# Moving layer 1's two gate groups of modulation tiles out of layer 0's output stage

## The chip, the cores and the metric

One core of one Trainium2 chip runs one launch of the kernel. The time is device microseconds of that core. TensorE (PE) multiplies, ScalarE (ACT) and VectorE (DVE) read PSUM and prepare operands, GpSimd (POOL) adds a few sums, and SyncE (SP) issues the weight transfers.

## What is computed

The reference has two blocks. The first has two layers with this skeleton, of which the change touches the modulation:

```
for l in range(2):
    m = silu(c) @ ada_w[l] + ada_b[l]          # 1024 -> 3072: shift, scale, gate
    sh, sc, gt = split(m, 3)
    h = rms_norm(x, norm_pre[l]) * (1 + sc) + sh
    z = h @ w_in[l]                            # q, k, v, hyena, gmlp, gates
    y_a = differential attention(q, k, v) with axial rope
    y_b, y_c = hyena long convolution, gmlp
    out = (sum of sel_i * (gated_i @ w_branch[i])) @ w_out[l]
    x = x + gt * rms_norm(out, norm_post[l])
```

x has 256 tokens of 1024 features; a context of 256 tokens is carried through layer 0 as well, and layer 1 still makes keys and values from it. The modulation is a product of two vectors (c and c_ctx) with a 1024 x 3072 matrix. The second block (sparse attentions, a feed-forward part, a last gated projection) comes after both layers.

## The kernel before

**The stream of tiles.** All weights lie in one array of tiles of 128 x 1024 fp32 (512 KB) in the order in which they are used. `plan()` names each tile (kind, layer, index, PSUM banks), and each engine's program walks the same list. SP loads tile t into one of four slots (`raw`, slot t mod 4). A tile of ordinary weights is split: ACT copies it to `whi` (L1194), DVE makes `wlo = raw - whi` (L1711), and PE does three matmuls for each product (L417 to L419). ACT runs three tiles ahead of its own reading of results, DVE two. A slot is free for tile t when tile t-4 has its `wlo`:

```
elif t >= second:
    sp.wait_ge(*self.at("used" if self.tiles[t - RAW].kind == "ada" else "tile_lo", t - RAW))
sp.dma_start(self.raw_tile(t), self.ins["stream"][t])
```

SP works in the order of the stream, so that a tile that waits holds back all behind it.

**Modulation tiles** (kind "ada") are used raw by PE, without a split (L506: the two vectors are the weights, the tile is the moving operand). Four tiles make one group g of 512 of the 3072 columns; groups 0 and 1 are the shift, 2 and 3 the scale, 4 and 5 the gate. When the fourth is done, ACT copies the bank to `rows` (L1217), PE transposes it (`pe_turn`, L598), and DVE adds the strips into `mod` (`dve_turned`, L1837). When groups 4 and 5 are there, `dve_mod_gate` (L2159, L2160) finishes the gate, which layer 1 needs only in its own output stage.

**Layer 0's output stage** walks eight "wout" tiles, each of 24 matmuls of 512 columns. Behind tiles 0 and 1 come two tiles each of layer 1's group 4, behind tiles 3 and 4 two each of group 5 (`WOUT_ADA`), and `pe_turn` follows at tiles 2 and 5. The same stage holds the filter of layer 1: two hidden products (L656), the taps (L666), and DVE's and ACT's part of it.

**Between the layers** (`pe_cross`, `act_cross`, `dve_cross`): PE sums the squares of the new x (L748), ACT takes the root, DVE the reciprocal (L2223), and then h comes k by k (eight k) over three steps: DVE L2238, ACT L1505 (`h_hi`), DVE L2244 (`h`). PE multiplies four query tiles by it (`pe_cross_queries`) as the k arrive, and then four key tiles over both halves. DVE does the `wlo` of the third query tile at the head of this stage and that of the fourth in `dve_cross_h(0)`, after its fourth h sum (`if s == 0 and k == 3: self.dve_lo()`); those of the four key tiles come after it.

**Layer 1's attention**: DVE turns keys and queries (`dve_rope`, L1976 to L1979) in three parts, with one `dve_tiles(1)` after each, PE does scores of unit 0 (L816), DVE the maxima (L1984 to L1986), ACT the exponentials (`act_exps`, L1387), and then eight units go on, each with two "hy" tiles of 24 matmuls of 256 columns in between. ACT takes each such result out at L1244, DVE finishes it at L1729 and L1730, and only then does the weights of the unit (L1997 to L2002), which PE transposes (L842).

Of the kernel before, what the change touches and what calls it, by code (L numbers as in the profile page):

```python
# [41 lines left out]
WOUT_ADA = {0: (4, (0, 1)), 1: (4, (2, 3)), 3: (5, (0, 1)), 4: (5, (2, 3))}  # L42
# [52 lines left out]
def plan():  # L95
# [33 lines left out]
    for l in range(DEPTH):  # L129
        n = ALL if l == 0 else TOK  # L130
        if l == 0:
            for g in FRONT_ADA:
                ada(0, g)
        for kind in ("q", "k") if l else ("k", "q"):
# [86 lines left out]
class Kernel:  # L221
    SLOTS = [0, 1, 2, 3, 6, 7] + list(range(8, 16))
    SPREAD = (4, 5, 10, 11, 12, 13)
    FRONT_GROUPS = tuple((0, g) for g in FRONT_ADA)
    LATE_ADA = ((0, 4), (0, 5), (1, 0), (1, 1))
# [259 lines left out]
    def pe_tile(self, T):  # L485
# [8 lines left out]
        if kind == "ada":  # L494
# [4 lines left out]
            if q == 0 and (T.l, g) in ASIDE:  # L499
# [87 lines left out]
    def pe_turn(self, l, g):  # L587

        pe, rows = self.pe, self.rows(l, g)
        if (l, g) in ASIDE:  # L590
            b = self.M[3]
            if (l, g) == ASIDE[1]:
                pe.wait_ge(*self.at("turned", *ASIDE[0]))
        else:
# [5 lines left out]

    def ada_bank(self, T):
        return self.M[2] if (T.l, T.j[0]) in ASIDE else self.G[T.use % 4]
# [181 lines left out]
    def pe_cross(self):  # L784

        queries, keys = self.tiles[self.pe_next:self.pe_next + 4], self.tiles[self.pe_next + 4:self.pe_next + 8]
# [32 lines left out]
    def pe_attention(self, l):  # L819
        pe, units = self.pe, self.units(l)  # L820
        n = len(units)
        pe.wait_ge(*self.at("roped", l, 7))
        self.pe_scores(l, 0)
        self.pe_tiles(1)
        for u in range(n):
# [24 lines left out]
            if i == 1:  # L850
                pe.wait_ge(*self.at("wt", l, u))
                if u == 1:
                    pe.wait_ge(*self.at("evac", self.tiles[self.first["v", l]].use + 3))
                if u > 1:
# [79 lines left out]
    def pe_block1(self, l):  # L934
# [15 lines left out]
        for o in range(KT):  # L950
            self.pe_tiles(1)
            if l == 0 and o in (2, 5):
                self.pe_turn(1, 4 + o // 3)
            if l == 0 and o in WOUT_ADA:
                self.pe_tiles(2)
# [231 lines left out]
    def act_hi(self):  # L1187

        t, act = self.act_next, self.act
        if t < len(self.tiles) and self.tiles[t].kind != "ada":  # L1190
            act.wait_ge(*self.raw_landed(t))
            if t >= FRONT + SPLIT:
                act.wait_ge(*self.at("used", t - SPLIT))
# [10 lines left out]
    def act_tile(self, T):  # L1204
        act, kind, l, j, n = self.act, T.kind, T.l, T.j, T.n
        b = self.G[T.use % 4]
        if kind == "ada":
            g, q = j
            if q == 3:
# [109 lines left out]

    def act_down_low(self, i):  # L1320
# [181 lines left out]
    def act_cross_h(self, s):  # L1502
        for k in range(KT):
            self.act.wait_ge(*self.at("h_sum", 1, s, k))
            self.act.activation(self.hi(k, s), self.tmp[:, (0, 1, 3, 4)[k % 4], self.half(s)], ACT.Identity, bias=self.mods[1][:, k, s:s + 1]).then_inc(*self.mark("act_half", "h_hi", 1, s, k))  # L1505

    def act_cross(self):
# [6 lines left out]
        self.act_hi()  # L1514
# [8 lines left out]
        for i in range(4):  # L1523
            for k in CROSS_SQ[i]:
                self.act_cross_sq(1, k)
            self.act_tiles(1)
        act.wait_ge(*self.at("summed", ("res", 0, 1), KT - 1))
# [3 lines left out]
    def act_block1(self, l):  # L1531
# [23 lines left out]
        for o in range(KT):  # L1555
            if o == 5 - 4 * l:
                act.activation(self.stat[:, 38:39], self.c["eps"], ACT.Sqrt, bias=self.c["zero"])
            self.act_tiles(3 if l == 0 and o in WOUT_ADA else 1)
# [273 lines left out]
    def dve_turned(self, l, g):  # L1832
        aside = (l, g) in ASIDE
        bank = self.M[3] if aside else self.G[self.extra["ada", l, g] % 4]
# [153 lines left out]
    def dve_attention(self, l):  # L1988
# [4 lines left out]
        self.dve_tiles(1)  # L1993
        for u in range(n):
# [12 lines left out]
            if l:  # L2007
                self.dve_tiles(FILL[1][u])
            elif u % 2:
# [145 lines left out]
    def dve_mod_gate(self, l):  # L2155

        v, mod, b = self.dve, self.mods[l], self.both(f"ada_b{l}", 24)
        v.wait_ge(*self.at("evac", self.extra["ada", l, 5]))
# [87 lines left out]
    def dve_cross(self):  # L2246
# [12 lines left out]
        for _ in range(4):  # L2259
# [5 lines left out]
    def dve_block1(self, l):  # L2265
        v, n = self.dve, TOK if l else ALL
        if l:
            self.dve_tiles(6, split=False)
# [26 lines left out]
        for o in range(KT):  # L2295
            self.dve_tiles(3 if l == 0 and o in WOUT_ADA else 1)
            if l == 0 and o in (0, 2):
                self.dve_hidden(1, o // 2)
            if l == 0 and o in (2, 5):
                self.dve_turned(1, 4 + o // 3)  # L2300
            if l == 0 and o == 5:
# [3 lines left out]
                self.dve_mod_gate(1)  # L2305
# [496 lines left out]
```

## Time and profile before

| | us |
|---|---|
| median of 3 runs (1432.98 to 1436.71) | 1434.15 |
| profiled execution, its own time | 1432.28 |
| its span, first to last instruction | 1431.0 |
| PE busy | 1374.4 (96%) |
| DVE busy | 936.4 (65%) |
| ACT busy | 686.8 (48%) |
| mean granted TensorE clock | 0.987 |

The profiled execution took 1.3 us more than its span, and the median of the runs is 1.9 us above it. In a row of the timeline stand start, duration, engine, line and operation, what it writes and reads, how many in a row, and in brackets the idle time before it and what ended that. PE's matmuls overlap, so that the distance from start to start tells what one costs, and not its duration.

### The profile page before, as it was taken

Reading aid. Unit: us, or ns where it says so; the run is one execution under the profiler, and the core shown is the slowest. Engines: PE = TensorE matmul, PEld = TensorE weight load, DVE = VectorE, ACT = ScalarE, POOL = GpSimd, SP = SyncE. Lnnn points to the kernel's source line nnn. Section 1 sums busy time; section 2 is a strip of 40 time slices with the busy share of each in tenths; the row PEclk is TensorE's granted clock in tenths of the full one; section 3 lists DMA queues with packets and bytes.
Section 4 is the critical chain, followed back from the end, with each engine's and each line's share of the span. In section 5 each row is a group of like instructions: output and inputs, shape, how many; then the busy total and the mean of one; then the engine's idle time right before and its main releaser. Section 6 shows DMA issues by size and latency. Waiting matters only on the chain.

```text
span 1431.0 us, 20879 instructions
## 1 busy us (share of the span) xinstructions
PE 1374.4 (96%) x8316; PEld 1162.7 (81%) x8316; DVE 936.4 (65%) x1688; ACT 686.8 (48%) x1190; POOL 41.6 (3%) x50
## 2 busy tenths in 40 slices
PE   6999999999999999989999999988999999999998
PEld 3676677778888887669789899987889989888878
DVE  6564664876333434398876787657877777888556
ACT  5434554134322232545455454455556746666445
POOL 0000000000000000200000000010000002000001
PEclk9999999999999999999999999998999999999999
DMA  9431351254322233513234455544543345555552
GB/s 366 169 103 59 139 197 48 71 176 144 103 90 101 91 106 104 193 59 104 88 119 133 155 174 191 180 163 137 191 133 119 104 149 175 192 191 192 198 170 74
DMA packets 57937, 202.21 MB, mean 141 GB/s; under 512 B 6288, under 2 KB 9680, under 8 KB 57840
## 3 DMA queue, kind: packets, MB, share of 16 engines
q1 hardware_dynamic: 55712, 194.27, 40.1%
q0 software_dynamic: 1760, 6.12, 1.3%
q8 instruction: 66, 1.08, 0.3%
q10 hardware_dynamic: 368, 0.48, 0.1%
q14 instruction: 31, 0.25, 0.1%
HBM read 199.80 MB, written 1.05 MB: 140 GB/s over the span
## 4 chain that ended last, share of the span: by engine, by line
PE 83%; DVE 10%; ACT 3%; DMA 2%; issue 1%; SPq 0%; DVEq 0%; ACTq 0%
PE gemm_bank L417 16%; PE gemm_bank L418 15%; PE gemm_bank L419 15%; PE misc_bank L417 4%; PE misc_bank L418 4%; PE misc_bank L419 4%; PE misc_bank L428 3%; PE gemm_bank L428 3%; DVE wlo L1711 2%; PE gemm_bank L573 1%; PE misc_bank L429 1%; PE gemm_bank L429 1%; PE misc_bank L573 1%; PE misc_bank L857 1%; PE gemm_bank L506 1%; PE misc_bank L816 1%
## 5 line engine op out<-in xcount | busy, mean ns | idle before, releaser
L1711 DVE TENSOR_TENSOR wlo<-raw,whi 128x1024 fp32r<-128x1024 f32 x316 | 383.1, 1223 | 74.6 <-ACT whi L1194 71.2
L1194 ACT ACTIVATE whi<-raw 128x1024 fp32r<-128x1024 f32 x316 | 332.6, 1055 | 163.3 <-PE gemm_bank L419 95.9
L417 PE MATMUL gemm_bank<-halves,wlo 128*128 128x256 f32 (+1 forms) x1152 | 376.4, 327 | 16.9 <-DVE halves L2244 4.2
L418 PE MATMUL gemm_bank<-halves,whi 128*128 128x256 f32 (+1 forms) x1152 | 361.4, 314 | 0.0
L419 PE MATMUL gemm_bank<-halves,whi 128*128 128x256 f32 (+1 forms) x1152 | 361.1, 313 | 0.0
L417 PEld LDWEIGHTS gemm_bank<-halves,wlo 128*128 128x128 f32 x1152 | 223.5, 194 | 40.6 <-issue 17.3
L419 PEld LDWEIGHTS gemm_bank<-halves,whi 128*128 128x128 f32 x1152 | 223.9, 194 | 12.0
L418 PEld LDWEIGHTS gemm_bank<-halves,whi 128*128 128x128 f32 x1152 | 224.2, 195 | 11.1 <-issue 0.7
L417 PE MATMUL gemm_bank<-arena_r,wlo 128*128 128x512 f32 (+1 forms) x320 | 108.4, 339 | 0.9 <-DVE wlo L1711 0.9
L419 PE MATMUL gemm_bank<-arena_r,whi 128*128 128x512 f32 (+1 forms) x320 | 107.8, 337 | 0.0
L418 PE MATMUL gemm_bank<-arena_r,whi 128*128 128x512 f32 (+1 forms) x320 | 107.8, 337 | 0.0
L417 PE MATMUL misc_bank<-halves,wlo 128*128 128x512 f32 (+1 forms) x288 | 102.0, 354 | 0.0
L418 PE MATMUL misc_bank<-halves,whi 128*128 128x512 f32 (+1 forms) x288 | 102.0, 354 | 0.0
L419 PE MATMUL misc_bank<-halves,whi 128*128 128x512 f32 (+1 forms) x288 | 102.0, 354 | 0.0
L1746 DVE SCALAR_TENSOR_TENSOR tmp<-tmp,gemm_bank 128x512 f32<-128x512 f32 (+1 forms) x28 | 16.1, 574 | 97.3 <-ACT tmp L1263 97.3
L1263 ACT ACTIVATE tmp<-misc_bank 128x512 f32<-128x512 f32 (+1 forms) x36 | 19.0, 527 | 121.4 <-PE misc_bank L419 121.4
L417 PEld LDWEIGHTS gemm_bank<-arena_r,wlo 128*128 128x128 f32 x320 | 60.8, 190 | 10.2 <-DVE wlo L1711 2.6
L419 PEld LDWEIGHTS gemm_bank<-arena_r,whi 128*128 128x128 f32 x320 | 60.8, 190 | 6.3
L418 PEld LDWEIGHTS gemm_bank<-arena_r,whi 128*128 128x128 f32 x320 | 60.8, 190 | 6.1
L428 PE MATMUL gemm_bank<-halves,whi 128*128 128x512 f32 x176 | 62.2, 395 | 0.0
L428 PE MATMUL misc_bank<-halves,whi 128*128 128x512 f32 x176 | 62.1, 394 | 0.0
L418 PEld LDWEIGHTS misc_bank<-halves,whi 128*128 128x128 f32 x288 | 54.6, 189 | 7.5
(417 smaller groups left out, 2261.5 us busy)
## 6 DMA issues: line engine op xcount, KB each, us to landing
raw<-in_stream SPq DMA_DIRECT2D x348, 512.0 KB, 3.3
arena<-in_stream SPq DMA_DIRECT2D x16, 512.0 KB, 12.6
x<-in_x SPq DMA_DIRECT2D x1, 1024.0 KB, 6.5
x<-in_ctx SPq DMA_DIRECT2D x1, 1024.0 KB, 9.4
y<-in_hy_decay POOLq DMA_DIRECT2D x2, 512.0 KB, 4.2
arena<-in_gm_ws POOLq DMA_DIRECT2D x2, 512.0 KB, 6.5
const_b<-in_const_b POOLq DMA_DIRECT2D x1, 635.0 KB, 6.3
y<-in_hy_w POOLq DMA_DIRECT2D x2, 256.0 KB, 3.7
```

Source lines behind the costliest of these rows:

```text
L417: mm(out, w_lo, r_hi, start=first, stop=False)
L418: mm(out, w_hi, r_lo, start=False, stop=False)
L419: return mm(out, w_hi, r_hi, start=False, stop=last)
L428: self.pe.matmul(bank[:, :], hi[:, c], self.hi_lo(k, s), start=(k == 0), stop=False)
L429: m = self.pe.matmul(bank[:, 0:TOK], lo[:, c], self.hi(k, s), start=False, stop=(k == KT - 1))
L506: m = pe.matmul(bank[c:c + 32, :], self.cond_w[:, 2 * q + kk, :], raw[:, kk * BR:(kk + 1) * BR], start=(q < 2), stop=(q >= 2), tile_positi ...
L573: pe.matmul(self.out_banks[o][:, :], hi[:, c], self.ah_al[:, j, :], start=(j == 0), stop=False)
L816: mm = pe.matmul(self.M[m][:, 0:nkeys], self.Q[r, h, q], self.K[r, h, k_off:k_off + nkeys], start=True, stop=True)
L1194: act.activation(self.whi[:, t % SPLIT, :], self.raw_tile(t), ACT.Copy).then_inc(*self.mark("tile_hi", "tile_hi", t))
L1263: act.activation(self.tmp[:, e % 2, 0:n], self.M[e][:, 0:n], ACT.Tanh, scale=0.5).then_inc(*self.mark("act_sel", "sel_tanh", T.use))
L1711: dve.tensor_tensor(self.wlo[:, t % SPLIT, :], self.raw_tile(t), self.whi[:, t % SPLIT, :].bitcast(F32), ALU.subtract).then_inc(*self.mark ...
L1746: self.own(dve.scalar_tensor_tensor(th, th, 1.0, b[:, 0:n], ALU.add, ALU.mult))
```

## The change

The pattern of `WOUT_ADA` (eight modulation tiles) goes. Group (1, 4), now `CROSS_ADA`, stands in the stream behind the four query tiles of layer 1 and before its keys. PE does its four tiles between the first sums and the queries, ACT copies the bank in `act_cross_h(0)` after the fourth `h_hi`, PE turns it after the keys, DVE reduces it after the second part of the rope. Group (1, 5), now `SCORE_ADA`, stands behind the value tiles: three tiles before the first hy tile, the fourth behind it. PE does three before it waits for the rope, and the fourth between the scores of unit 0 and the first hy tile; then it turns the group. ACT copies that bank after the exponentials of unit 0. DVE reduces it in unit 0 and then does the gate. Both groups are turned through misc banks. ACT's and DVE's look-ahead steps count the new places.

```
-WOUT_ADA = {0: (4, (0, 1)), 1: (4, (2, 3)), 3: (5, (0, 1)), 4: (5, (2, 3))}
+CROSS_ADA, SCORE_ADA, SCORE_ADA_LEAD = (1, 4), (1, 5), 3
...
+            if l and kind == "q":
+                for q in range(4):
+                    add("ada", 1, (CROSS_ADA[1], q), 0, 0)
+                    tiles[-1].use = cross_use
         rows("v", l, 4, ALL)
+        if l:
+            for q in range(SCORE_ADA_LEAD):
+                add("ada", 1, (SCORE_ADA[1], q), 0, 0)
         for m in range(12):
             add("hy", l, m, n, 1)
+            if l and m == 0:
+                for q in range(SCORE_ADA_LEAD, 4):
+                    add("ada", 1, (SCORE_ADA[1], q), 0, 0)
...
             add("wout", l, o, n, 1)
-            if l == 0 and o in WOUT_ADA:
-                ada_part(1, *WOUT_ADA[o])
...
     def pe_cross(self):
...
         for k in range(KT):
             self.pe_cross_sum(0, k)
+        for T in moving:
+            self.pe_tile(T)
         self.pe_cross_queries(queries)
         for i, side in CROSS_KEYS:
             self.pe_cross_keys(keys[i], side, (i, side) == (0, 1))
-        self.pe_next += 8
+        self.pe_turn(*CROSS_ADA)
+        self.pe_next += 12
...
     def pe_attention(self, l):
+        if l:
+            self.pe_tiles(SCORE_ADA_LEAD)
+        if l:
+            pe.wait_ge(*self.at("turned", *CROSS_ADA))
         pe.wait_ge(*self.at("roped", l, 7))
         self.pe_scores(l, 0)
-        self.pe_tiles(1)
+        if l:
+            lead = self.tiles[self.pe_next]
+            for T in self.tiles[self.pe_next + 1:self.pe_next + 5 - SCORE_ADA_LEAD]:
+                self.pe_tile(T)
+            self.pe_tile(lead)
+            self.pe_next += 5 - SCORE_ADA_LEAD
+            self.pe_turn(*SCORE_ADA)
+        else:
+            self.pe_tiles(1)
...
+    def act_beside(self, l, g):
+
+        T = next(T for T in self.tiles if T.kind == "ada" and T.l == l and T.j == (g, 3))
+        self.act.wait_ge(*self.at("used", T.t))
+        self.act.wait_ge(*self.at("ada_turn", l, g - 1))
+        m = self.act.activation(self.rows(l, g), self.ada_bank(T)[:, :], ACT.Copy)
...
     def act_attention(self, l):
+        if l:
+            for _ in range(3):
+                self.act_hi()
+            self.act_tiles(SCORE_ADA_LEAD, split=False)
         self.act_exps(l, 0)
-        self.act_tiles(1)
+        if l:
+            self.act_beside(*SCORE_ADA)
+            self.act_tiles(2)
+        else:
+            self.act_tiles(1)
...
             self.act.activation(self.hi(k, s), self.tmp[:, (0, 1, 3, 4)[k % 4], self.half(s)], ACT.Identity, bias=self.mods[1][:, k, s:s + 1]).then_inc(*self.mark("act_half", "h_hi", 1, s, k))
+            if s == 0 and k == 3:
+                self.act_beside(*CROSS_ADA)
...
     def dve_attention(self, l):
         self.dve_maxima(l, 0)
         self.dve_tiles(1)
+        if l:
+            self.dve_tiles(4 - SCORE_ADA_LEAD, split=False)
...
             if l:
                 self.dve_tiles(FILL[1][u])
+                if u == 0:
+                    for _ in range(4 - SCORE_ADA_LEAD):
+                        self.dve_lo()
+                    self.dve_turned(*SCORE_ADA)
+                    self.dve_mod_gate(1)
...
     def dve_block1(self, l):
             self.dve_rope(l, a, b)
+            if l and a == 3:
+                self.dve_turned(*CROSS_ADA)
             self.dve_tiles(1)
...
-        if l == 0:
-            self.dve_tiles(1)
+        self.dve_tiles(SCORE_ADA_LEAD if l else 1)
```

## Rows read from the trace of the kernel before

**Rows 1.** The page: span, and the chain that ended last by engine

```profile
span 1431.0 us, 20879 instructions
...
PE 83%; DVE 10%; ACT 3%; DMA 2%; issue 1%; SPq 0%; DVEq 0%; ACTq 0%
```

**Rows 2.** Timeline of PE in layer 0's output stage

```profile
566.97 1.06 PE L506 MATMUL gemm_bank<-raw,cond_w 128*32 128x512 f32 x8
567.96 0.64 PE L656 MATMUL misc_bank<-const_b 33*64 33x256 f32 x2
...
574.20 1.07 PE L506 MATMUL gemm_bank<-raw,cond_w 128*32 128x512 f32 x8
576.17 0.50 PE L417 MATMUL gemm_bank<-arena_r,wlo 128*128 128x512 f32 x1 [0.91 <-DVE wlo L1711]
...
581.75 0.60 PE L598 MATMUL gemm_bank<-const_a 128*128 128x128 f32 x4
```

**Rows 3.** Timeline of PE between the layers

```profile
623.41 5.37 PE L748 MATMUL misc_bank<-tmp,const_a 128*128 128x256 f32 x16
632.93 0.55 PE L417 MATMUL gemm_bank<-halves,wlo 128*128 128x256 f32 x1 [4.15 <-DVE halves L2244]
...
637.87 0.42 PE L418 MATMUL gemm_bank<-halves,whi 128*128 128x256 f32 x1
...
638.24 0.28 PE L417 MATMUL gemm_bank<-halves,wlo 128*128 128x256 f32 x1
```

**Rows 4.** Timeline of DVE between the layers

```profile
617.35 1.22 DVE L1711 TENSOR_TENSOR wlo<-raw,whi 128x1024 fp32r<-128x1024 f32 x1
...
633.89 1.22 DVE L1711 TENSOR_TENSOR wlo<-raw,whi 128x1024 fp32r<-128x1024 f32 x1
```

**Rows 5.** Windows: PE busy, its granted clock, DMA share, GB/s

```profile
622.00:624.00 2.00, 2.00 (x7) 1.00 0.00 0
...
634.00:636.00 2.00, 2.00 (x11) 0.50 0.00 0
636.00:638.00 2.00, 2.00 (x11) 0.50 0.82 268
```

**Rows 6.** All transfers into the raw slots, 560 to 740 us

```profile
DMA to landing us min/median/max: 3.1/3.7/7.3
```

**Rows 7.** The chain that ended last, near 568 us

```profile
568.43 5.35 DMA raw<-in_stream
```

**Rows 8.** Timeline of ACT between the layers

```profile
635.94 0.51 ACT L1505 ACTIVATE halves<-tmp,mod 128x256 fp32r<-128x256 f32 x1 [1.42 <-DVE tmp L2238]
```

**Rows 9.** Timeline of PE at layer 1's first scores

```profile
698.79 1.32 PE L816 MATMUL misc_bank<-arena 64*128 64x512 f32 x4 [3.44 <-DVE arena L1979]
```

**Rows 10.** Timeline of DVE: a strip sum, then around layer 1's first units

```profile
586.75 0.17 DVE L1837 TENSOR_REDUCE mod<-gemm_bank 128x8 f32<-128x32 f32 x1
...
691.26 1.22 DVE L1711 TENSOR_TENSOR wlo<-raw,whi 128x1024 fp32r<-128x1024 f32 x1
...
713.93 0.48 DVE L1729 SCALAR_TENSOR_TENSOR arena<-gemm_bank,const_b,arena 128x255 f32<-128x255 f32 x1 [1.79 <-ACT arena L1244]
```

**Rows 11.** Timeline of ACT: output stage, then layer 1's first units

```profile
577.09 0.60 ACT L1217 ACTIVATE const_a<-gemm_bank 128x512 f32<-128x512 f32 x1
577.71 1.28 ACT L1335 ACT_TABLE_LOAD   x1
579.00 0.42 ACT L1335 ACTIVATE tmp<-tmp 64x256 f32<-64x256 f32 x1
...
698.86 1.28 ACT L1387 ACT_TABLE_LOAD   x1
701.75 0.69 ACT L1387 ACTIVATE tmp<-misc_bank,stat 128x512 f32<-128x512 f32 x1 [1.60 <-DVE stat L1986]
...
703.09 1.05 ACT L1194 ACTIVATE whi<-raw 128x1024 fp32r<-128x1024 f32 x1
...
711.05 0.69 ACT L1387 ACTIVATE tmp<-misc_bank,stat 128x512 f32<-128x512 f32 x1 [1.41 <-DVE stat L1986]
```

More of the change, by code:

```diff
@@ L133, in plan @@
                 ada(0, g)
+        if l:
+            cross_use, uses = uses, uses + 1
         for kind in ("q", "k") if l else ("k", "q"):
@@ L498, in pe_tile @@
             raw, bank = self.raw_tile(T.t), self.ada_bank(T)
-            if q == 0 and (T.l, g) in ASIDE:
+            if q == 0 and (T.l, g) == SCORE_ADA:
+                pe.wait_ge(*self.at("kern", 1, 1))
+            elif q == 0 and (T.l, g) in ASIDE:
                 if (T.l, g) == ASIDE[1]:
@@ L784, in pe_cross @@
     def pe_cross(self):
-        queries, keys = self.tiles[self.pe_next:self.pe_next + 4], self.tiles[self.pe_next + 4:self.pe_next + 8]
+        queries, moving, keys = (self.tiles[self.pe_next + 4 * i:self.pe_next + 4 * i + 4] for i in range(3))
         for k in range(KT):
             self.pe_cross_sum(0, k)
+        for T in moving:
+            self.pe_tile(T)
         self.pe_cross_queries(queries)
@@ L1192, in act_hi @@
             if t >= FRONT + SPLIT:
-                act.wait_ge(*self.at("used", t - SPLIT))
+                held = t - SPLIT
+                while held > FRONT + SPLIT and self.tiles[held].kind == "ada":
+                    held -= SPLIT
+                act.wait_ge(*self.at("used", held))
             act.activation(self.whi[:, t % SPLIT, :], self.raw_tile(t), ACT.Copy).then_inc(*self.mark("tile_hi", "tile_hi", t))
@@ L1208, in act_tile @@
             g, q = j
-            if q == 3:
+            if q == 3 and (l, g) not in self.BESIDE:
                 act.wait_ge(*self.at("used", T.t))
@@ L1318, in act_tile @@
             act.activation(self.y[:, j, 0:TOK], self.y[:, j, 0:TOK], ACT.Tanh, scale=0.5).then_inc(*self.mark("act_ple", "ple_tanh", j))
+    def act_beside(self, l, g):
[3 more added lines that the diff above has]
+        m = self.act.activation(self.rows(l, g), self.ada_bank(T)[:, :], ACT.Copy)
+        if (l, g) == SCORE_ADA:
+            m.then_inc(*self.mark("act_rows", "rows", l, g))
+            return
+        m.then_inc(*self.mark("act_evac", "evac", T.use))
+        self.also("rows", l, g)
     def act_down_low(self, i):
@@ L1513, in act_cross @@
         self.act_tap_root(1)
-        self.act_hi()
+        for _ in range(5):
+            self.act_hi()
         for k in range(KT):
@@ L1557, in act_block1 @@
                 act.activation(self.stat[:, 38:39], self.c["eps"], ACT.Sqrt, bias=self.c["zero"])
-            self.act_tiles(3 if l == 0 and o in WOUT_ADA else 1)
+            self.act_tiles(1)
             if l == 0 and o in (1, 3):
@@ L1833, in dve_turned @@
         aside = (l, g) in ASIDE
-        bank = self.M[3] if aside else self.G[self.extra["ada", l, g] % 4]
+        aside = aside or (l, g) in self.BESIDE
+        bank = self.turn_bank(l, g) if aside else self.G[self.extra["ada", l, g] % 4]
         self.dve.wait_ge(*self.at("ada_turn", l, g))
@@ L2258, in dve_cross @@
             self.dve_cross_new(1, k)
-        for _ in range(4):
+        for _ in range(8):
             self.dve_lo()
@@ L2650, in _layout @@
             tiles.append(_columns(w[:, c:c + 512]))
+            if l and c:
+                ada(1, CROSS_ADA[1], CROSS_ADA[1] + 1)
         tiles.append(_rows(w[:, 512:1024]))
@@ L2661, in _layout @@
         else:
-            tiles.append(hy)
+            at = len(tiles)
+            ada(1, SCORE_ADA[1], SCORE_ADA[1] + 1)
+            moving = tiles.pop(at)
+            tiles += [moving[:SCORE_ADA_LEAD], hy[0:1], moving[SCORE_ADA_LEAD:], hy[1:]]
             early = _columns(w[:, 5632:5632 + 2 * KEPT_SEL * P])
@@ L2679, in _layout @@
         wout = _columns(i["w_out"][l])
-        if l == 0:
-            at = len(tiles)
-            ada(1, 4, 6)
-            both, done = tiles.pop(at), 0
-            for o in range(KT):
-                tiles.append(wout[o:o + 1])
-                if o in WOUT_ADA:
-                    tiles.append(both[done:done + 2])
-                    done += 2
-        else:
-            tiles.append(wout)
+        tiles.append(wout)
     w = i["w_in_2"][0]
```

30 lines of the change are left out of this document (20 added, 10 removed).

## The prediction

> **What bounds the kernel now.** I read the page first. PE has 83% of the chain that ended last [rows 1] and 96% of the span: what PE need not do, or need not wait for, is what counts. The eight moved tiles are PE work, and they still have to be done. So the change can only gain by putting them where PE stands idle, and the next views are timelines of PE at the place they leave and at the two places they go to. They leave layer 0's output stage, where PE runs without a gap but for one of 0.91 us [rows 2]. Between the layers PE stands for 4.15 us from 628.78 us on, until DVE has the first h [rows 3], and then runs at half its clock up to about 638.1 us: the granted clock is 0.50 of 2.4 GHz, that is the 1.2 GHz level [rows 5], and matmuls come every 0.21 us instead of every 0.12. At layer 1's first scores PE stands for 3.44 us, until the rope is done [rows 9]. Last I looked at what the moved steps wait for at the new places: DVE's order between the layers [rows 4], the transfers [rows 5 to 7], and ACT and DVE around the first units of the attention [rows 10, 11]. The reader is to see that both gaps are large enough for the work, and that the transfers are not ready for them.
>
> **What the output stage gives back.** One pair of tiles takes 0.99 us from its start to the start of what follows, another 1.06 us and then 0.91 us of waiting for a `wlo`, which is late because transfers of three tiles come in a bunch behind the pair (5.35 us for the last of them) [rows 2, 7]. Four pairs are 4.2 us, the wait 0.9, the two turns 0.45 each (0.60 us long, of which the last part lies under the next matmul), and each return to the weight tiles about 0.1 (the first matmul of one takes 0.50 us), five times. Sum 6.5 us; bounds 5.6 (the wait comes back in another form) and 6.8 (turns at their full length). DVE's and ACT's filter work of this stage only becomes less crowded. I take 6.5 off.
>
> **The group between the layers.** PE takes its four tiles right after the last sum, in order, and before the queries. Each needs its transfer. A slot is free when tile t-4 has its `wlo`, and the t-4 of the group's fourth tile is the fourth query tile. Its `wlo` is the one that DVE does after the fourth h sum: 633.89 to 635.11 us [rows 4]. The windows agree: the three transfers let go by the `wlo` of 617.35 and earlier end before 622, then nothing moves for seven windows of 2 us, and the next tile (today the fourth key tile, in the very slot) runs at 636 to 638 us [rows 4, 5]. So the fourth tile of the group lands no earlier than 635.11 + 3.1 = 638.2 us, by the shortest landing there is [rows 6]. PE does three tiles in the gap, until about 630.4, and then stands almost 8 us instead of 4.15. The fourth tile takes half a pair, 0.53 us, and twice that at half clock: the queries begin at 638.3 + 1.05 = 639.35 instead of 632.93, 6.4 us later. As the stretch at half clock was 5.2 us long and 1.05 of it now lies before the queries, they get back 0.5. Net +5.9. Bounds: +5.0 (clock back early) and +8.1 (landing 5.35 instead of 3.1, as there are three key tiles issued right behind [rows 7]).
>
> Behind it on ACT: the copy of the bank stands after the fourth `h_hi` and waits for the fourth tile. The slot it was given is real (ACT idles 1.42 us there while DVE does the `wlo` [rows 8]), but now ACT is held until 639.4, and h of k = 4 to 7 follows some 3.5 us later, at about 641 to 643 us. PE asks for the fifth k after sixteen steps of three matmuls, about 647 us, so nobody waits. The x of the second half moves by 3.5 too and stays ahead of PE's sums, which move by 5.9. The turn after the keys (0.45) falls into PE's gap before the scores.
>
> **The group at the scores.** Two things help: DVE has one `wlo` (1.22) less before the rope is done and one strip sum (0.17) more, so that the rope is ready 1.0 us earlier, at 697.8 on the old scale [rows 9, 10]; and three tiles (1.6 us) and the turn (0.45) lie in PE's 3.44 us of idleness. What counts from there is not PE. From one unit to the next, ACT's exponentials wait for DVE's maxima and DVE waits for ACT's hy result (1.79 us idle) [rows 10, 11], a ring of the two engines in which PE is just in time. So I ask when the first exponential starts: 701.75 today [rows 11]. In the new order ACT must first make `whi` of the second hy tile. That tile's slot held the second of the three group tiles, which PE uses at about 696.9 (695.35, the turn, two tiles); one transfer is ahead of it, and one takes 1.9 us at 268 GB/s [rows 5]. It lands at about 696.35 + 3.1 + 1.9 = 701.4. Then come `whi` (1.05) and the table load (1.28), which is hidden in a wait today [rows 11] and is not any more: 703.7. That is +1.9. Bounds: +0.6 (landing 3.1 after its own issue, 700.0) and +2.7 (landing 5.35 after it).
>
> The copy of this group (0.60, as at 577.09 [rows 11]) goes between the exponentials and the first hy result and is mostly paid for by a `whi` and a PE wait that stood there: +0.1, bounds 0 and 0.6. In unit 0 DVE makes up the `wlo` it left out, sums the strips and finishes the gate, after the hy result and before the weights: 1.22 + 0.17 and two more short ones, 1.65 us, on the ring, and behind the idle time, not in it. Bounds 0 and 1.75. Together +3.65, bounds +0.6 and +5.0; I take 3.5, as some of the `wlo` may be caught up in the units behind.
>
> **The skill on the table load.** At 577.71 the load begins 0.02 us after the copy before it has ended and takes 1.28, and the function starts at 579.00 [rows 11]. The Trainium skill's page "ScalarE: Activation LUTs", section "What ACT_TABLE_LOAD costs", charges 1283 ns for the load and some 1380 ns of drain, 2.66 us for a switch. By that, as an estimate, the sum below would be 1.4 us higher. The trace has no room for a drain there, so the row decides.
>
> **Sum.** -6.5 + 5.9 + 3.5 = +2.9 us on the profiled execution of 1432.28, which makes 1435.2; the median of the runs shown lies 1.9 higher, so 1437.0 against 1434.15. Moved PSUM banks (every later use counts three fewer) and the shallower look-ahead I set at nothing, as each wait goes by its own number; together they may be worth 1 us either way. I call 0.3%, 4.3 us, what a measurement of this kernel can tell from no change.
>
> **The rivals.**
> - *The tiles fit into the gap between the layers.* It holds if the fourth tile has landed by 628.8. Then that place costs nothing and the clock may stay up (about -1.1): -6.5 - 1.1 + 3.5 = -4.1, 1430.0. It needs its transfer issued ten microseconds before its slot is free; the windows are empty there [rows 5]. With the attention also at its low bound it would be -7. Faster by over 0.3% comes from here and from unseen gains: 0.10.
> - *The attention costs almost nothing* (its low bound, as the second hy tile lands quickly and DVE's extra work is caught up): -6.5 + 5.9 + 0.7 = +0.1, 1434.3. For it: PE's gap there really is filled and the rope is 1 us earlier. Against it: the ring has no slack that a row shows. 0.22.
> - *The transfers come late.* The fourth tile lands after 5.35 us, not 3.1, as the one at 568.43 did [rows 7]: +2.2, sum +5.1, 1439.3. It decides from 1.4 us more on. Against it: it is the first in its bunch, not the last. With the other high bounds (second hy tile, half clock), slower by over 0.3%: 0.27.
> - *The load holds ACT for twice its row* (2 x 1.28 us, as if something unseen followed it): +1.3, sum +4.2, 1438.3, just at the bound. At 579.00 nothing unseen follows [rows 11]; 0.04, inside the last case. This is the case in which the page's rule would hold.
>
> **How the numbers follow.** Forecast as summed, within 0.3% and slightly slower: 0.41; attention at nothing 0.22; late transfers and high bounds 0.27; faster 0.10. So faster 0.10, same 0.63, slower 0.27. Range: from 1431.0 (half-way into the faster case) to 1441.5 (late transfer and attention's high bound, +7.3 at most); it leaves out about 2 in 10.
>
> **What the profile after would show.** Right: PE idle from about 624 to 632 (6.5 us earlier than on the old scale), ended by a transfer, then a single modulation tile, then the queries at half clock; ACT waiting in the copy after the fourth `h_hi`; wlo of the fourth query tile followed 3.1 us later by the landing; in the output stage no 0.91 us wait; before layer 1's first exponential a wait of ACT on a transfer, then `whi`, then the load in the open; unit 1 of the attention longer by 1.5 us. Wrong: PE's idleness between the layers under 4 us, or the first exponential within 0.5 us of the end of the maxima. The forecast goes wrong most easily by the landings, each of which stands on the critical path and spreads from 3.1 to 7.3 us.

## The result and the profile after

| | before | after |
|---|---|---|
| median (runs) | 1434.05 (20) | 1437.14 (20) |
| range | 1432.19 to 1439.18 | 1434.99 to 1443.5 |
| profiled execution, span | 1432.28, 1431.0 | 1438.47, 1437.2 |
| PE, DVE, ACT busy | 1374.4, 936.4, 686.8 | 1376.6, 936.0, 686.7 |
| mean granted clock of the profile | 0.987 | 0.985 |

The ratio is 1.002, with a 95% interval from 1.001 to 1.0029: the change costs 3.1 us, inside the 0.3% that the forecast called no change, and on the side that it named (+2.9). The median came out at 1437.14 where 1437.0 was forecast.

The page of the changed kernel, span and chain by engine, beside [rows 1]:

```profile
span 1437.2 us, 20880 instructions
...
PE 85%; DVE 8%; ACT 3%; DMA 2%; issue 1%; ACTq 0%; SPq 0%; DVEq 0%
```

Nothing in the page tells where 3 us went. What tells it is a handful of instructions that both kernels have, one at each border of the places that the change touches, and the distances between them. These are the marks, from the timelines (start, duration, engine, line, operation). Of the kernel before: PE's passage to the last branch products (A), DVE's pooled sum near the end of the output stage (B), DVE's last h (C), its last rope sum (D), and ACT's exponential of unit 2 (F); that of unit 0 (E) stands in [rows 11].

```profile
550.56 0.39 PE L417 MATMUL misc_bank<-halves,wlo 128*128 128x512 f32 x1
...
615.50 1.21 DVE L1882 TENSOR_TENSOR arena<-arena 128x1024 f32<-128x1024 f32 x1
...
660.71 0.48 DVE L2244 SCALAR_TENSOR_TENSOR halves<-tmp,mod,halves 128x256 fp32r<-128x256 f32 x1 [0.18 <-ACT halves L1505]
...
698.31 0.42 DVE L1979 TENSOR_TENSOR arena<-arena,tmp 128x256 f32<-128x256 f32 x1
...
719.86 0.69 ACT L1387 ACTIVATE tmp<-misc_bank,stat 128x512 f32<-128x512 f32 x1 [2.14 <-DVE stat L1986]
```

The same of the changed kernel:

```profile
551.60 0.39 PE L428 MATMUL misc_bank<-halves,wlo 128*128 128x512 f32 x1
...
609.87 1.23 DVE L1945 TENSOR_TENSOR arena<-arena 128x1024 f32<-128x1024 f32 x1 [5.35 <-ACT arena L1391]
...
661.45 0.48 DVE L2318 SCALAR_TENSOR_TENSOR halves<-tmp,mod,halves 128x256 fp32r<-128x256 f32 x1 [0.18 <-ACT halves L1563]
...
698.39 0.42 DVE L2042 TENSOR_TENSOR arena<-arena,tmp 128x256 f32<-128x256 f32 x1
...
724.38 0.69 ACT L1437 ACTIVATE tmp<-misc_bank,stat 128x512 f32<-128x512 f32 x1 [2.13 <-DVE stat L2049]
```

Every kernel's profile, in us between the marks (A is the time from the start; the last column is what is left of the span behind F). The other rows are the experiments below:

| | A | A to B, output stage | B to C, between layers | C to D, rope | D to E | E to F | behind F |
|---|---|---|---|---|---|---|---|
| before | 550.56 | 64.94 | 45.21 | 37.60 | 3.44 | 18.11 | 711.1 |
| after | 551.60 | 58.27 | 51.58 | 36.94 | 6.16 | 19.83 | 712.8 |
| after, again | 553.07 | 58.27 | 52.22 | 36.92 | 6.12 | 19.84 | 710.3 |
| low part early | 553.77 | 58.27 | 44.71 | 36.94 | 6.06 | 19.83 | 710.9 |
| fourth tile late | 551.41 | 58.28 | 46.40 | 36.95 | 6.09 | 19.85 | 710.8 |
| one group, scores | 553.10 | 62.76 | 44.78 | 36.47 | 6.15 | 19.85 | 711.4 |
| one group, between | 550.51 | 62.03 | 52.05 | 37.70 | 4.29 | 18.73 | 712.5 |
| high part later | 550.36 | 58.27 | 52.07 | 36.95 | 3.33 | 20.86 | 712.3 |
| high part later, again | 551.01 | 58.27 | 51.13 | 36.96 | 3.33 | 20.80 | 710.4 |
| low part in the gap | 550.42 | 58.27 | 52.45 | 36.94 | 6.09 | 18.12 | 712.7 |
| copy later | 553.70 | 58.28 | 51.95 | 36.96 | 6.15 | 19.83 | 709.7 |
| two mended | 551.11 | 58.27 | 45.88 | 36.91 | 6.14 | 18.12 | 711.9 |
| all three mended | 550.51 | 58.28 | 46.20 | 36.96 | 3.33 | 19.08 | 711.0 |
| all three, again | 553.30 | 58.27 | 44.70 | 36.93 | 3.34 | 19.07 | 711.3 |

From before to the first profile of the changed kernel the columns give -6.67, +6.37, -0.66, +2.72 and +1.72, together +3.5. The other four repeat to 0.1 us in the second profile of the changed kernel; B to C does not, and the first and last columns, where the kernels do the same work, scatter by 3.4 and 3.1 us over all profiles. The profiles before and after differ by 6.2 us, of which 1.0 is there before anything changed (551.60 against 550.56) and 1.7 comes behind F. Reading two spans against each other would have told nothing.

**Between the layers** the changed kernel's PE answers to [rows 3]:

```profile
623.44 1.91 PE L519 MATMUL gemm_bank<-raw,cond_w 128*32 128x512 f32 x12
633.68 1.92 PE L519 MATMUL gemm_bank<-raw,cond_w 128*32 128x512 f32 x4 [8.33 <-DMA raw<-in_stream]
635.53 0.58 PE L428 MATMUL gemm_bank<-halves,wlo 128*128 128x256 f32 x1
```

Three tiles lie in the gap, then PE stands 8.33 us for a transfer, does one tile, and begins the queries. DVE's `wlo` of the fourth query tile, which lets that transfer go, stands where [rows 4] had it, after the fourth h sum:

```profile
628.62 1.22 DVE L1773 TENSOR_TENSOR wlo<-raw,whi 128x1024 fp32r<-128x1024 f32 x1
...
636.68 0.48 DVE L2318 SCALAR_TENSOR_TENSOR halves<-tmp,mod,halves 128x256 fp32r<-128x256 f32 x1 [5.26 <-ACT halves L1563]
```

It ends at 629.84, and the tile starts 3.84 us later. The second row is the fifth h, which waits for ACT, and ACT for the copy of the bank (beside [rows 8]):

```profile
635.65 0.60 ACT L1363 ACTIVATE const_a<-gemm_bank 128x512 f32<-128x512 f32 x1 [6.41 <-PE gemm_bank L519]
```

The windows (PE busy, its clock, DMA share, GB/s at the end of a row) show the empty transfer lines up to the `wlo`, as in [rows 5], and the clock at its 1.2 GHz level from about 629.8 to 636.6 us:

```profile
626.00:628.00 2.00, 0.00 (x0) 0.00 (x0) 1.76 (x5) 0.96 (x3) 0.00 (x0) 1.00 0.00 0
628.00:630.00 2.00, 0.00 (x0) 0.00 (x0) 2.00 (x4) 0.96 (x2) 0.00 (x0) 0.95 0.00 0
630.00:632.00 2.00, 0.00 (x0) 0.00 (x0) 1.42 (x4) 0.00 (x0) 0.00 (x0) 0.50 0.61 145
...
634.00:636.00 2.00, 2.00 (x6) 0.47 (x3) 0.00 (x0) 0.35 (x1) 0.00 (x0) 0.50 1.03 418
636.00:638.00 2.00, 2.00 (x16) 2.00 (x16) 1.32 (x4) 1.45 (x4) 0.00 (x0) 0.84 0.88 283
```

**At the scores** PE's 3.44 us of idleness [rows 9] are 0.57 now; three tiles lie in them, and the fourth waits 0.88 us for its transfer:

```profile
696.48 1.91 PE L519 MATMUL misc_bank<-raw,cond_w 128*32 128x512 f32 x12
698.96 1.13 PE L841 MATMUL misc_bank<-arena 64*128 64x512 f32 x4 [0.57 <-DVE arena L2042]
700.98 1.05 PE L519 MATMUL misc_bank<-raw,cond_w 128*32 128x512 f32 x4 [0.88 <-DMA raw<-in_stream]
```

That does not help, since ACT comes late (beside [rows 11]):

```profile
702.17 1.06 ACT L1232 ACTIVATE whi<-raw 128x1024 fp32r<-128x1024 f32 x1 [3.25 <-DMA raw<-in_stream]
703.25 1.28 ACT L1437 ACT_TABLE_LOAD   x1
704.55 0.69 ACT L1437 ACTIVATE tmp<-misc_bank,stat 128x512 f32<-128x512 f32 x1
...
713.84 0.69 ACT L1437 ACTIVATE tmp<-misc_bank,stat 128x512 f32<-128x512 f32 x1 [1.51 <-DVE stat L2049]
```

DVE had its maxima done at 701.69; ACT waits for the second hy tile, makes its high part, and only then loads the table. Behind the hy result of unit 0 DVE does what it was spared (beside [rows 10]):

```profile
701.52 0.17 DVE L2049 TENSOR_SCALAR stat<-stat 128x2 f32<-128x2 f32 x1
...
716.72 0.48 DVE L1791 SCALAR_TENSOR_TENSOR arena<-gemm_bank,const_b,arena 128x255 f32<-128x255 f32 x1 [1.79 <-ACT arena L1282]
717.24 0.48 DVE L1792 SCALAR_TENSOR_TENSOR arena<-gemm_bank,const_b,arena 128x255 f32<-128x255 f32 x1
717.64 1.22 DVE L1773 TENSOR_TENSOR wlo<-raw,whi 128x1024 fp32r<-128x1024 f32 x1
718.77 0.19 DVE L1900 TENSOR_REDUCE mod<-misc_bank 128x8 f32<-128x32 f32 x1
719.06 0.18 DVE L2233 TENSOR_TENSOR mod<-mod,const_a 128x16 f32<-128x16 f32 x1
719.27 0.18 DVE L2234 TENSOR_TENSOR mod<-mod,const_a 128x16 f32<-128x16 f32 x1
```

From 717.64 to the next step of the unit (a reciprocal, at 719.37) that is 1.73 us, behind the idle time.

### The profile page after: what moved, and what is told of

Same layout as the page of the kernel before. It is cut to its first block, busy times and chain, and to the rows that moved or that the text cites. A ratio compares the mean times of both kernels' runs of the same rounds, so it can differ in the third digit from the quotient of the medians.

```text
span 1437.2 us, 20880 instructions
## 1 busy us (share of the span) xinstructions
PE 1376.6 (96%) x8316; PEld 1162.8 (81%) x8316; DVE 936.0 (65%) x1688; ACT 686.7 (48%) x1190; POOL 39.9 (3%) x50
## 3 DMA queue, kind: packets, MB, share of 16 engines
q0 software_dynamic: 1760, 6.12, 1.3%
HBM read 199.80 MB, written 1.05 MB: 140 GB/s over the span
## 4 chain that ended last, share of the span: by engine, by line
PE 85%; DVE 8%; ACT 3%; DMA 2%; issue 1%; ACTq 0%; SPq 0%; DVEq 0%
PE gemm_bank L428 16%; PE gemm_bank L430 16%; PE gemm_bank L429 16%; PE misc_bank L428 4%; PE misc_bank L429 4%; PE misc_bank L430 4%; PE misc_bank L439 3%; PE gemm_bank L439 3%; DVE wlo L1773 2%; PE gemm_bank L586 1%; PE misc_bank L586 1%; PE misc_bank L440 1%; PE gemm_bank L440 1%; DMA raw<-in_stream 1%; PE misc_bank L896 1%; PE misc_bank L841 1%
## 5 line engine op out<-in xcount | busy, mean ns | idle before, releaser
L428 PEld LDWEIGHTS misc_bank<-halves,wlo 128*128 128x128 f32 x288 | 54.5, 189 | 7.5
```

What stands on the lines that cost most here:

```text
L428: mm(out, w_lo, r_hi, start=first, stop=False)
```

## The experiments

The theory: the output stage gives back 6.7 us; the group between the layers costs 5.9 to 7.2 (by the profile) because its fourth transfer waits for a late `wlo`; the group at the scores costs 2.1 by the late first exponential and 1.7 by DVE's catch-up. Each edit is against the changed kernel, but for the two with one group, whose excerpt shows the difference from the kernel before. The ratios are to the kernel before, run beside each: its median was 1434.6 beside the first four experiments and 1433.7 beside the others, so that a difference across the two sets is taken from the ratios or from these medians and not from the raw times.

**Low part early.** DVE makes the fourth query tile's low part before the h chain begins.

```
         self.dve_cross_rstd(("out", 0), 0)
         self.dve_tap_rs(1)
+        self.dve_lo()
...
-            if s == 0 and k == 3:
-                self.dve_lo()
```

> The changed kernel, but DVE does the wlo of the fourth query tile right behind the first reciprocal between the layers instead of after the fourth h sum. My theory (the group's fourth tile is late because its slot is freed by that wlo): the fourth tile lands before the sums end, PE's idle time between the layers falls from 8.3 us to about 2 us in place of 8.3, the queries start 6.6 us earlier, and all is some 7 us faster than the changed kernel: about 3.9 us below the kernel before (ratio 0.997). DVE's chain up to the first h is 1.2 us longer, which is in that sum. Rival (PE waits there mainly for DVE's h and ACT's copy, and the transfer is only the last of several): the gain is under 2 us, ratio 1.001 or more.

Measured: 1430.45 (12 runs), ratio 0.9971 (0.996 to 0.9982). Timeline of PE: all sixteen records of the group run before the queries, and PE stands 2.30 us where it stood 8.33.

```profile
626.74 1.92 PE L519 MATMUL gemm_bank<-raw,cond_w 128*32 128x512 f32 x16
630.97 0.36 PE L428 MATMUL gemm_bank<-halves,wlo 128*128 128x256 f32 x1 [2.30 <-DVE halves L2316]
```

B to C is 44.71, 0.5 under the kernel before, and the clock stays at 2.4 GHz. The queries start 1.5 us later behind B than in the kernel before (18.93 against 17.43), and from the first query to C it is 2.0 us less (25.78 against 27.78). The low part ends 7.2 us behind B (619.26) instead of 20.0 us (629.84).

**Fourth tile late.** The transfer is left as it is, but PE does the fourth tile inside the queries, and ACT copies behind the eighth `h_hi`.

```
             T = tiles[i]
+            if step == 9:
+                self.pe_tile(late)
...
-        for T in moving:
+        for T in moving[:3]:
             self.pe_tile(T)
...
-            if s == 0 and k == 3:
+            if s == 0 and k == 7:
                 self.act_beside(*CROSS_ADA)
```

> The changed kernel, but PE does the group's fourth tile inside the queries, before their tenth step, and ACT copies the bank after the eighth h_hi. The wlo and the transfer stay as late as they are. My theory: the transfer no longer holds the queries up; some 5 us faster than the changed kernel, about 1.9 us below the kernel before (ratio 0.9987), with an idle time of 2 to 3 us before the queries and under 1.5 us at the fourth tile. If the late wlo cost time in another way than through the queries' start, this stays near the changed kernel (ratio 1.002) while e1 gains.

Measured: 1432.73 (12 runs), ratio 0.9987 (0.9975 to 1.0). PE stands 2.31 us before the queries. B to C is 46.40, 1.7 us more than with the early low part: the tile still waits 0.74 us for its transfer, and being alone it takes 0.98 us to the next matmul (`x4` at 632.90):

```profile
632.90 1.05 PE L519 MATMUL gemm_bank<-raw,cond_w 128*32 128x512 f32 x4 [0.74 <-DMA raw<-in_stream]
```

Both ways out of the same wait gain, so it is that wait which costs, and not the presence of the group between the layers.

**One group at the scores; one group between the layers.** In both, group (1, 4) stays in layer 0's output stage, two tiles each behind its tiles 0 and 1, and group (1, 5) moves: in the first kernel to the scores, in the second between the layers, with the gate finished after the attention.

```
-CROSS_ADA, SCORE_ADA, SCORE_ADA_LEAD = (1, 4), (1, 5), 3
+WOUT_ADA = {0: (4, (0, 1)), 1: (4, (2, 3))}
+MOVED, SCORE_ADA_LEAD = (1, 5), 3
```

(These lines are the same in both; `MOVED` stands in the place of `SCORE_ADA` in the first and of `CROSS_ADA` in the second.)

> Only group (1, 5) is moved, to the scores; group (1, 4) stays in layer 0's output stage. By the terms of the prediction: the stage gives back 2.8 us (two pairs and a turn; the 0.91 us wait stays), the attention costs 3.7: about +0.9 us against the kernel before (ratio 1.0006). If the attention's cost was overrated (rival: it hides), -2 us (0.9985).

> Only one group, named (1, 5) here, is moved, to the place between the layers; group (1, 4) stays in the output stage; the gate is finished after the attention. By the terms of the prediction: -2.8 us in the stage, +6.0 between the layers: about +3.2 us against the kernel before (ratio 1.0022). If the loss of the changed kernel comes from the attention instead, -2 us or better (0.9985).

Measured: 1434.69, ratio 1.0002 (0.9991 to 1.0012) for the scores alone, 12 runs; 1439.26, ratio 1.0025 (1.0013 to 1.0037) for between the layers alone, 12 runs. That is +0.1 us where +0.9 was expected, and +4.7 where +3.2 was. The main prices stay where the theory has them. With the scores alone B to C is 44.78, near the 45.21 before, and D to E and E to F are those of the changed kernel (6.15 and 19.85). With the other alone B to C is 52.05. Each gets its share of the output stage, 2.2 and 2.9 us, less than half of 6.67: PE's wait for a `wlo`, 0.91 us before, is still there in both, and longer (1.77 and 1.06 us).

Between the layers alone, D to E and E to F are also longer than before, by 0.85 and 0.62 us, though no group stands at the scores. There PE's gap is empty again, and its clock is at 1.2 GHz from about 702.4 to 709.2 us, through all scores of unit 0 and into the hy tile:

```profile
702.86 2.08 PE L834 MATMUL misc_bank<-arena 64*128 64x512 f32 x4 [3.16 <-DVE arena L2016]
```

The same four took 1.32 us in the kernel before [rows 9]. No term of the expectation has these 1.5 us.

**High part later.** ACT makes the second hy tile's high part behind unit 0's exponentials. It ran twice, the second time beside the changed kernel itself.

```
         if l:
-            for _ in range(3):
+            for _ in range(2):
                 self.act_hi()
             self.act_tiles(SCORE_ADA_LEAD, split=False)
         self.act_exps(l, 0)
         if l:
+            self.act_hi()
             self.act_beside(*SCORE_ADA)
```

> The changed kernel, but ScalarE makes the high part of unit 0's second tile of the hy weights behind unit 0's exponentials instead of before them. Theory (the first exponential starts 2 us later because ScalarE stands idle for that tile's transfer, makes its high part in 1.06 us and only then loads the table): the first exponential starts some 1.8 us earlier than in the changed kernel, the tile itself is needed only by unit 1, and nothing else moves. Against the change's measured 3.1 us over the kernel before that leaves +1.3 us, a ratio of 1.0009 (1.0002 to 1.0016). Rival (the first exponentials are not what the end of unit 0 waits for; the whole price of the scores lies with VectorE's catch-up): the ratio stays at 1.002.

> The changed kernel itself, once more, as the anchor of this call: 1.002 (1.001 to 1.003) of the kernel before. In its trace the steps from stage to stage come out as in the first profile to within 0.1 us, except the stretch from the pooled sum of layer 0 to the last h, which holds the return of TensorE's clock and spread from 51.6 to 52.5 us in four traces.

> The changed kernel with only the high part of unit 0's second hy tile behind the exponentials. Its trace showed 1.8 us less up to unit 2's exponentials, its median only 0.7 less than the changed kernel's. If the trace is right, the median beside the changed kernel of this same call is 1.8 us lower, ratio to the kernel before 1.0008 (1.0 to 1.0016). If the 1.8 us are given back behind the attention, it is within 0.5 us of the changed kernel's, ratio 1.002.

Measured: 1436.43 (12 runs), ratio 1.0018 (1.0006 to 1.0029); again 1436.56 (11 runs), 1.0016 (1.0007 to 1.0026), beside 1437.41 (11 runs), 1.0028 (1.0017 to 1.0038) for the changed kernel. In both profiles the first exponential starts as early as foreseen. The load is back under the wait for the maxima, as in [rows 11]:

```profile
697.91 1.28 ACT L1437 ACT_TABLE_LOAD   x1
700.70 0.69 ACT L1437 ACTIVATE tmp<-misc_bank,stat 128x512 f32<-128x512 f32 x1 [1.51 <-DVE stat L2050]
```

D to E falls by 2.8, E to F rises by 1.0 (the expectation had "nothing else moves"), and F is 1.8 us nearer. The medians of the two kernels run beside each other differ by 0.85 us. That lies between the two ways that the expectation names, and with intervals of some 1.4 us either way it excludes neither. The granted clock gives a lead. It was 0.985 on the mean over this kernel's 23 executions and 0.987 over the changed kernel's 31, and within each of the two the longer executions have the lower clock, by 0.7 to 1.3 us for each 0.001. So TensorE stood at its lower level for longer here, which would take back part of the gain; that it did was argued from these means and not tried. Why they did is open.

**Low part in the gap.** DVE does unit 0's catch-up before the hy result, where it stands idle.

```
-                self.dve_tiles(FILL[1][u])
                 if u == 0:
-                    for _ in range(4 - SCORE_ADA_LEAD):
+                    for _ in range(5 - SCORE_ADA_LEAD):
                         self.dve_lo()
                     self.dve_turned(*SCORE_ADA)
                     self.dve_mod_gate(1)
+                self.dve_tiles(FILL[1][u], split=u > 0)
```

> The changed kernel, but VectorE does unit 0's catch-up (the low part of the second tile of the hy weights, the two strips and the gate of the group, 1.65 us together) before the hy result of that unit, where it stands idle for TensorE, instead of after it. Theory (these 1.65 us lie on the chain that leads to unit 1's statistics): the work falls into idle time, and the exponentials of unit 2 start some 1.65 us earlier than in the changed kernel; ratio to the kernel before 1.001 (1.0004 to 1.0018). Rival (VectorE has slack in unit 1, and all of the scores' price is the late first exponential): the ratio stays at 1.002. A second way to miss: the low part waits for ScalarE's high part of the same tile, and then the hy result itself is late by what is left of that wait; then the gain is under 1 us.

Measured: 1434.57 (12 runs), ratio 1.0009 (0.9997 to 1.0021). Timeline of DVE: two low parts in a row, the strips and the gate, and the hy result directly behind, where [rows 10] had 1.79 us of idleness.

```profile
713.35 2.35 DVE L1773 TENSOR_TENSOR wlo<-raw,whi 128x1024 fp32r<-128x1024 f32 x2
715.62 0.18 DVE L1900 TENSOR_REDUCE mod<-misc_bank 128x8 f32<-128x32 f32 x1
...
716.36 0.48 DVE L1791 SCALAR_TENSOR_TENSOR arena<-gemm_bank,const_b,arena 128x255 f32<-128x255 f32 x1
```

E to F is 18.12, that of before to 0.01. The catch-up was on the path and is off it, and ACT's copy of the group, which is still there, costs nothing in this step.

**Copy later.** ACT's copy between the layers stands behind the eighth `h_hi`; PE's order is that of the changed kernel.

```
-            if s == 0 and k == 3:
+            if s == 0 and k == 7:
                 self.act_beside(*CROSS_ADA)
```

> The changed kernel, but ScalarE's copy of the group between the layers is made four query steps later (behind the halves of step 7 instead of step 3); TensorE's order is unchanged. In the changed kernel ScalarE stands idle 6.41 us in front of that copy, and halves 4 to 7 are late by it. Theory (the queries are late because TensorE stands before the fourth tile; ScalarE's hold hurts nobody): halves 4 to 7 are ready some 3.5 us earlier, the queries start when they did, and the ratio stays at 1.002 (1.0013 to 1.0029). Rival (the halves held back by ScalarE are what keeps the queries late, by VectorE's chain of halves): the kernel is some 3 us faster, ratio 1.000.

Measured: 1437.81 (6 runs), ratio 1.0029 (1.0017 to 1.0041). DVE has the last h of the first half at 635.69 us, before PE's first query at 637.06, so the halves are early by far, and nothing is gained: B to C is 51.95, and PE waits 7.75 us for the transfer. ACT's idleness of 6.41 us in front of the copy costs nothing.

**Mended.** Low part early, high part later and low part in the gap together, twice; and once without the high part.

> The changed kernel with three edits together: VectorE's low part of the fourth query tile right behind the first reciprocal (as in the first run, which by itself gave 0.9971), the high part of unit 0's second hy tile behind the exponentials (worth 1.8 us by my theory), and unit 0's catch-up on VectorE before the hy result (worth 1.65 us). If the three prices add, because they lie one after another on the one chain that sets the end, the time is 1430.45 - 1.8 - 1.65 = 1427.0 us, a ratio of 0.9947 (0.9935 to 0.996). If the gains in the scores overlap (both shorten the way to the same statistics, and only the longer counts), it is 1428.6 us, 0.9958. If neither counts, 0.9971.

> The changed kernel with VectorE's low part of the fourth query tile early and unit 0's catch-up before the hy result, but with the high part of the second hy tile where the change put it: 1430.45 - 1.7 = 1428.8 us, ratio 0.996 (0.995 to 0.997). If the late high part costs 1.8 us in this setting, it is 1.8 us above the kernel with all three edits; if it is given back later, the two are equal.

> All three edits, once more beside the others: 1427.0 us, ratio 0.9950 (0.994 to 0.996), 1.8 us under the kernel with two of them.

Measured: 1427.24 (6 runs), ratio 0.9956 (0.9942 to 0.997), and again 1427.3 (5 runs), 0.9956 (0.9943 to 0.9969); with two edits 1430.15 (11 runs), 0.998 (0.9968 to 0.9993). The version with all three beats both kernels, the one before by 6.4 us and the changed one by 10 us. In the profiles the prices of the two edits at the scores add: D to F is 25.89 us with the low part early alone, 24.26 with the low part in the gap as well, and 22.41 with all three, steps of 1.6 and 1.85, near the 1.8 of each alone. The times do not show this as plainly. The low part early is 4.15 us under the kernel before beside it, all three are 6.4, so the other two give 2.3 us, where their prices add to 3.45 and 1.85 would be the overlap that the expectation names; the raw medians, 1430.45 and 1427.24, would say 3.2, but the kernel before also ran 0.9 us faster beside the second. The two-edit kernel is 3.5 us under the kernel before, so that the low part in the gap, worth 2.2 us alone (3.1 less 0.9), shows nothing here, and the high part 0.85 alone and 2.85 here. Single medians of this kernel do not settle 1.5 us.

## Why the prediction was right

**Output stage: right.** -6.67 for -6.5, the same to 0.01 in every profile that has both groups out.

**The late fourth transfer: the mechanism right, the size near by luck.** Forecast +5.9, measured +6.37 in the first profile and +7.01 in the second. The mechanism is settled by the first two experiments. In the first profile two errors nearly cancel, +1.8 and -1.4; in the second they are +1.3 and -0.15. Of its terms:

- The queries start 25.66 us behind B, against 17.43 before: +8.2, not +6.4. The transfer took 3.84 us from the end of the `wlo` where 3.1, the shortest of [rows 6], was taken (3.26 to 3.35 in the six other profiles with this order between the layers); the `wlo` itself ended 0.36 later behind B than before. And the single tile took 1.85 us to the first query where 1.05 was: "the fourth tile takes half a pair" failed. The rows above show `x4` alone at full clock as 1.05 us, the same as the `x8` of a pair in [rows 2], and `x12` in 1.91, the same as `x16` in 1.92. The kernel gives a tile two of four column groups of 32, and the next tile the other two (`c = 32 * ((2 * q + kk) % 4)` and `tile_position=(0, c)`, q the tile and kk its half). So four records cost what eight cost, and nearly twice that at 1.2 GHz. The page "TensorEngine Tiling (Array Packing)" of the Trainium skill says, under "Key Properties", that different tiles of the array work in parallel; the trace agrees (8 records in 1.06 us, 4 in 1.05), and an odd tile out throws that half away.
- From the first query to C it is 25.92 us, against 27.78: -1.9, not -0.5. "The stretch at half clock was 5.2 us long and 1.05 of it now lies before the queries" took for granted that it would last as long past PE's return as before. In the first profile it did not: it ended 2.9 us behind PE's return and 1.1 into the queries, since most of it lay in the idle time. In the second it did: it ended in the 640 to 642 us window, 5.7 us behind PE's return and 3.9 into the queries, and from the first query to C it is 27.13 us, -0.65, as forecast:

```profile
634.00:636.00 2.00, 1.42 (x4) 0.19 (x4) 0.00 (x0) 0.00 (x0) 0.00 (x0) 0.50 0.91 344
636.00:638.00 2.00, 2.00 (x9) 1.58 (x8) 0.43 (x2) 1.39 (x3) 0.00 (x0) 0.50 1.02 363
638.00:640.00 2.00, 2.00 (x11) 2.00 (x10) 1.82 (x6) 1.02 (x2) 0.00 (x0) 0.50 0.76 287
640.00:642.00 2.00, 2.00 (x17) 2.00 (x17) 1.93 (x6) 0.49 (x2) 0.00 (x0) 0.92 0.08 31
```

**ACT's hold hurts nobody: right**, by the copy made later.

**The first exponential: right.** D to E +2.72, less the rope's 0.66, is +2.06 for +1.9; the rope came 0.66 earlier, not 1.0, as DVE's third `wlo` behind C waits 1.55 us for ACT's high part instead of 1.18. The load in the open took 1.28 us and the function started at once, 1.30 after it began, as its row said; the load itself began 0.02 behind the high part. The drain of 1380 ns that the Trainium skill's page "ScalarE: Activation LUTs" adds under "What ACT_TABLE_LOAD costs" is not there.

**DVE's catch-up: right; the copy: nothing.** +1.72 for 1.65 + 0.1, and with the catch-up in the gap and the copy still there it is +0.01. The 0.15 that was taken off for later catching up was not there. Scores together +3.8 for 3.5.

**The sum.** The steps make +3.5, or +4.1 with the second profile's; the medians say 3.1 and 3.7. The step from the profile to the median is where the arithmetic was lucky: the forecast put the profiled execution at 1435.2 and the median 1.9 above it, and the profile was 1438.47, 1.3 above its median. The right median rests on a base that scatters by some 3 us. That it came out within 0.2 us of the forecast is luck; that the two groups cost what the stage gives back and some 3 us more is not. The moved banks and the shallower look-ahead, set at nothing, have no column of their own, and no run tried them alone.

**The signs.** All that the prediction listed came: PE idle from 625.4 to 633.7 us until a transfer, one tile alone, ACT held in the copy, no wait of 0.91 us in the output stage, the load in the open behind a `whi`, and 10.54 us from the exponentials of unit 1 to those of unit 2 instead of 8.81.

**The rivals.** "The tiles fit into the gap" was given -1.1 us for its place; with the low part early the place gave -0.5 us where the clock stayed up, and cost 0.7 and 1.0 where it did not. "The attention costs almost nothing" is out, as the two edits at the scores take 1.8 us each off the path in the profiles. The transfer was late by 0.74 us more than its term, not by 2.2.

**What was not forecast.** Filling PE's gap at the scores also kept the clock up there. Before:

```profile
700.00:702.00 2.00, 2.00 (x11) 1.97 (x10) 1.75 (x4) 0.40 (x2) 0.00 (x0) 0.50 0.52 150
```

After:

```profile
700.00:702.00 2.00, 1.12 (x7) 0.19 (x5) 1.63 (x4) 0.00 (x0) 0.00 (x0) 1.00 1.01 385
```

Against this one profile of the kernel before it is worth 0.1 us: D to E is 3.33 with the high part later and 3.44 before, where the clock fell only behind the start of the scores. It can be worth more: with one group between the layers alone it fell earlier and stayed down longer, and D to F was 1.5 us longer than before.

## What to carry to other kernels

When work is moved into an engine's idle time, ask first when its transfer can start: find the instruction that frees its slot, and see whether it stands behind or before the gap. Here the gap was long enough and the work fitted, and one vector instruction of 1.22 us, done 12.7 us earlier, decided some 7 us. The same question stands before any copy: ACT's high part of a tile that only the next unit needs stood in front of the first exponentials, waited for its transfer, and held them up by 2.8 us, of which 1.0 was owed to the next unit anyway. And to judge an edit of a few us, compare distances between the same instructions in both traces, as the spans differ by as much for reasons that lie outside the edit; and check that the marks are the same instruction in every trace.

## What the runs showed of the hardware

- The length of the half-clock stretch is not fixed, for the same kernel and the same idle time. The kernel with the high part later ran twice, with 7.79 and 7.80 us of idleness in front of the fourth tile; the stretch at 1.2 GHz was 10.2 us the first time and 6.8 the second (from the shares of the windows), and B to C 52.07 and 51.13. Of the six profiles with the changed kernel's order on PE between the layers, two have 6.8 us (B to C 51.13 and 51.58) and four 10.2 (51.95 to 52.45). In the kernel before, with 4.15 us of idleness, it was 6.8 too.
- With 2.30 us of idleness in front of the queries the clock stayed at 2.4 GHz in two of four profiles (B to C 44.7 both times), and fell to 1.2 for 3.4 us in the other two (45.88 and 46.20).
- In front of the fourth tile, with the queues empty, a 512 KB transfer was in use 3.26 to 3.35 us behind the end of the `wlo` that freed its slot in six profiles, and 3.84 in the seventh.
- Parts of the program that no edit touched scatter by 3 us from profile to profile, up to A (550.4 to 553.8) as much as behind F (709.7 to 712.8).
